# A two-block network on one core: sums of the opening moved from TensorE to the vector engine, filter directions stacked into one matmul, spectra stored later

## The chip, the cores and the metric

One core of one Trainium2 chip. The metric is the device time of one execution in microseconds, as the median of several. The core has five engines that run their own instruction streams and wait for each other by semaphores: TensorE (PE), the vector engine (DVE), ScalarE (ACT), GpSimd (POOL), and the sync engine (SP), which here only issues transfers.

## The reference

The kernel computes a first block and then two more mixer layers on x of 256 x 2048. Of the first block this matters, all in float32:

```
mod = silu(c) @ w_ada + b_ada                       # 2048 x 12288: 12 groups of 1024 columns
sh1, sc1, g1, sh2, sc2, g2 = split(mod, 6)
h = x * (1 + sc1) + sh1
z = h @ w_in + b_in                                  # 2048 x 9216
z_u, z_v, z_h, z_g = split(z, ...)
# hyena filters, from constants and small weights alone
f = sin(freq * (feats @ w1 + b1)); f = sin(freq * (f @ w2 + b2))      # 256 x 64
f = (f @ w3).reshape(256, 2 directions, 2 orders, 1024) * window
k_spec = rfft of forward and reversed backward filter, for each order
```

The rest (gating, long convolutions with k_spec, MLP, two further layers) is untouched.

## The kernel before, in words

**Opening.** x needs sh1 and sc1, and these are groups 0 to 3 of mod. A group is read in 16 *chunks* of 128 x 1024 (512 KB), so the opening has chunks 0 to 63, and 64 to 191 follow beside the weights. Chunk j is multiplied with one column of silu(c) and added to an accumulator on the vector engine (`add_chunk`, L1050); some chunks (`PE_CHUNKS`) are summed on TensorE instead with single-column matmuls (`sum_chunk`, L630), and the first of a group on ScalarE. `reduce_chunks(i)` (L616) sums a group's accumulator over partitions on TensorE, and `bias(i)` makes it mod. Chunks lie in 8 slots up to chunk 31 and in 6 slots up to 63; the sync engine issues chunk j when the slot's previous chunk has been used, and everything behind it in its program waits with it.

**Filters.** Beside that, two sine layers (`sine_layer`, L1108, and a Sin on ScalarE), then the last layer: `both(0)` and `both(1)` (L1124) make the sum and the difference of the weights of the two directions on 64 partitions, 16 hidden-layer matmuls multiply (L663), `windowed(i)` (L1128) multiplies with the window, 16 groups of matmuls (L682) make the spectra, ScalarE copies them to `ksb` and POOL writes them in eight pieces of 512 KB to `kscr` in DRAM (L2254), from where they are read when the long convolutions need them. `wait_filters` makes the first short convolution wait for all eight, because it writes where they lay.

**Weights.** All weight matrices come as *halves* of 128 x 8 x 128 floats. ScalarE rounds half h to float32r (`hi(h)`, L1761), the vector engine makes the remainder (`lo(h)`, L1038), TensorE multiplies 8 *k tiles* a half, each as two matmuls (L586 with the rounded weights on x's two parts, L590 with the remainder). A column of w_in is 16 k tiles. The first three columns go by turns: k tiles 0 to 7 of each, with `reduce_chunks(3)` behind k = 4, then, in the order of `SECOND`, k tiles 8 to 15, whose x tiles wait for groups 2 and 3. Behind that, column after column: in step i the vector engine does two `lo`, `add_halves(i)` (L1189), for the first 24 columns a short convolution, and one `add_chunk`.

Of the kernel before, what the change touches and what calls it, by code (L numbers as in the profile page):

```python
# [15 lines left out]
P = 128  # L16
# [90 lines left out]
for _i in range(2):  # L107
# [29 lines left out]
PE_CHUNKS = (2, 4, 10, 18, 25, 57)  # L137
# [4 lines left out]
SUMS = [("chunk", 2), ("chunk", 4), ("chunk", 10), ("group", 0), ("chunk", 18), ("chunk", 25), ("group", 1),  # L142
        ("group", 2), ("chunk", 57), ("group", 3)] + [("group", i) for i in range(4, 12)]
# [42 lines left out]
def n_rest(k):  # L186
# [7 lines left out]
    "ada0 ada1 ada2 ada3 ada4 ada5 ada6 ada7 fin dft hw3 scr0 scr1 scr2 scr3 khat ws0 ws1 out "  # L194
# [11 lines left out]
    "fmm sine sin fwin both spmm spec "  # L206
# [49 lines left out]
def _build(nc, ctx, d, out):  # L256
# [6 lines left out]
    s_scr = (s.scr0, s.scr1, s.scr2, s.scr3)  # L263
# [58 lines left out]
    w3 = BFf[0:64, 0:4096]  # L322
# [5 lines left out]
    w2 = small[0:64, 320:384]  # L328
    hb = small[0:64, 384:387]
    ha, hn, h1, h2 = (small[0:64, 512 + 256 * i:768 + 256 * i] for i in range(4))  # L330
# [85 lines left out]
    n_ada = {17: 4, 33: 5, 49: 6, 65: 7}  # L416
# [64 lines left out]
    def wait_filters(w):  # L481
        for scr in s_scr:
            w.wait_ge(scr, 32)
# [14 lines left out]
    def sync_program(e):  # L498
# [31 lines left out]
        e.dma_start(w2, d["hy_w2"]).then_inc(s.fin, 16)  # L530
        e.dma_start(hb, d["hy_b"]).then_inc(s.fin, 16)
# [12 lines left out]
        w.wait_ge(s.fmm, 18)  # L544
# [11 lines left out]
        for h in range(H_M2[0]):  # L556
            weights(h + 7)
            paced = h < H_WO + 16 or h >= H_M1[0]
            if h % 2 and paced and at < 192:
                chunk(at)  # L560
                at += 1
# [10 lines left out]
    def tensor_program(e):  # L572
# [79 lines left out]
        w.wait_ge(s.fin, 64)  # L652
        e.matmul(ps[4][0:64, 0:256], w1, feats, start=True, stop=True).then_inc(s.fmm, 1)
        w.wait_ge(s.sin, 1)
        e.matmul(ps[4][0:64, 0:256], w2, h1, start=True, stop=True).then_inc(s.fmm, 1)
        sum_chunk(2)
        sum_chunk(4)
        w.wait_ge(s.sin, 2)
        for i in range(16):
            n, tt = i // 2, i % 2  # L660
            w.wait_ge(s.both, n // 4 + 1)
            w.wait_ge(s.fwin, i - 2)
            e.matmul(ps[3 + i % 3][:], h2[:, tt * P:tt * P + P], w3_both[n // 4][:, n % 4 * 512:n % 4 * 512 + 512],  # L663
                     start=True, stop=True).then_inc(s.fmm, 1)
            if i == 2:
                sum_chunk(10)
            if i == 8:
                reduce_chunks(0)
            if i == 10:
                sum_chunk(18)  # L670
            if i == 13:
                sum_chunk(25)
        reduce_chunks(1)
        w.wait_ge(s.dft, 16)
        w.wait_ge(s.fwin, 16)
        for i in range(16):
# [358 lines left out]
    def vector_program(e):  # L1035
# [71 lines left out]

        def sine_layer(i):  # L1108
            w.wait_ge(s.fin, 64)
            w.wait_ge(s.fmm, i + 1)  # L1110
            w.wait_ge(s.sin, i)
            sine.up(e.tensor_scalar(ha, ps[4][0:64, 0:256], hb[:, i:i + 1], hb[:, 2:3], ALU.add, ALU.mult))
            w.wait_ge(s.sine, sine.n)
            sine.up(e.tensor_scalar(hn, ha, 1.0 / TWO_PI, MAGIC, ALU.mult, ALU.add))
            w.wait_ge(s.sine, sine.n)
            sine.up(e.tensor_scalar(hn, hn, MAGIC, None, ALU.subtract))
            for c in (C1, C2, C3):
                w.wait_ge(s.sine, sine.n)
                sine.up(e.scalar_tensor_tensor(ha, hn, -c, ha, ALU.mult, ALU.add))
            w.wait_ge(s.sine, sine.n)  # L1120
            sine.up(e.tensor_scalar(ha, ha, 3.1415925, -3.1415925, ALU.min, ALU.max))


        def both(i):  # L1124
            w.wait_ge(s.hw3, 32)
            e.tensor_tensor(w3_both[i], w3[:, 0:2048], w3[:, 2048:4096], ALU.subtract if i else ALU.add).then_inc(s.both, 1)

        def windowed(i):  # L1128
            n, tt = i // 2, i % 2
            w.wait_ge(s.fmm, 2 + i + 1)  # L1130
            w.wait_ge(s.hw3, 32)
# [18 lines left out]
        for j in V_CHUNKS[:V_UPTO[63]]:  # L1150
            add_chunk()
            if j == 3:
                sine_layer(1)
            if j == 5:
                both(0)
            if j == 8:
                both(1)
# [8 lines left out]
            if j == 52:  # L1166
# [7 lines left out]
        for k in range(8, 16):  # L1174
            if k % 4 != 3:
                w.wait_ge(s.scale1, 2)
                w.wait_ge(s_x[k // 4], 16)
                e.tensor_scalar(XR[:, k, :], XR[:, k, :], mod[:, 16 + k:17 + k], mod[:, k:k + 1],
                                ALU.mult, ALU.add).then_inc(s.made_v, 1)
            if k >= 9:  # L1180
                made_low(k - 1)
            if k in (10, 11, 14):
                lo((10, 11, 14).index(k) + 4)
# [91 lines left out]
        for i, n in enumerate(N_IN):  # L1275
# [24 lines left out]
            add_chunk()  # L1300
            if i == 2:
# [456 lines left out]
    def scalar_program(e):  # L1758
# [61 lines left out]
        for k in range(8, 16):  # L1820
            if k % 4 == 3:
                make_tile(k)
            if k >= 9:
                high(k - 1)
            if k in (10, 11, 14):
                hi((10, 11, 14).index(k) + 4)
        high(15)

# [411 lines left out]
    def gpsimd_program(e):  # L2240
# [10 lines left out]

        for m in range(8):
            w.wait_ge(s.spec, 2 * m + 2)
            e.dma_start(kscr[m // 4, m % 4], ksb[:, m % 4, :]).then_inc(s_scr[m % 4], 16)  # L2254
            if m in (4, 5):
                made_low(3 * m - 11)
        for k in (7, 10, 13):
# [266 lines left out]
```

## Time and profile before

| | |
|---|---|
| median of 3 runs | 2688.38 us (2687.2 to 2692.71) |
| profiled execution | 2686.84 us, its span 2684.8 us |
| mean granted TensorE clock | 0.982 |
| TensorE busy | 2567.2 us, 96% of the span |
| vector engine busy | 1988.4 us, 74% |
| ScalarE, POOL busy | 1393.1 us, 802.2 us |
| transfers | 534.60 MB, mean 199 GB/s |

The span runs from the first to the last instruction. Busy time of an engine is the union of its instructions; what lies between them is waiting, or time in which its sequencer works. Matmuls are pipelined, so their ends are modelled, and TensorE that shows as busy all the time need not be at its peak.

### The profile page before, as it was taken

What the parts mean: (1) busy time and instruction counts of PE and PEld (TensorE: products, weight loads), DVE (VectorE), ACT (ScalarE), POOL (GpSimd) and SP (SyncE); (2) the same over time, 40 slices, a digit from 0 to 9 for tenths busy, and PEclk for the clock granted to TensorE, in tenths of its full rate; (3) what the DMA queues carried; (4) which work ended last, traced back from release to release, by engine and by line L of the source; (5) the groups of instructions that cost most, each with busy time, mean ns of one, the idle gap of its engine ahead of it and who ended that gap; (6) DMA issues with size and microseconds to landing.
All of it is one profiled execution on the core that took longest, in us unless ns stands there. A gap on an engine that the chain in (4) does not pass through costs nothing.

```text
span 2684.8 us, 42882 instructions
## 1 busy us (share of the span) xinstructions
PE 2567.2 (96%) x16652; PEld 2334.2 (87%) x16652; DVE 1988.4 (74%) x2574; ACT 1393.1 (52%) x2180; POOL 802.2 (30%) x764
## 2 busy tenths in 40 slices
PE   7799999999998999999999989999899999999979
PEld 4588888888986888888888879999789999999978
DVE  6779777768788785546555679898758788888855
ACT  0344334444455444435544466776556666766653
POOL 0100002002134410001111338875104556666630
PEclk9899999999999999999999989999999999999989
DMA  8978766787865886556555534444455444444434
GB/s 299 371 260 282 246 210 210 255 275 247 290 237 172 283 281 219 185 172 201 190 190 190 189 108 157 158 149 154 138 172 166 143 149 156 151 150 156 148 100 155
DMA packets 146770, 534.60 MB, mean 199 GB/s; under 512 B 16679, under 2 KB 16840, under 8 KB 146248
## 3 DMA queue, kind: packets, MB, share of 16 engines
q1 hardware_dynamic: 143320, 520.33, 57.4%
q0 software_dynamic: 3248, 11.54, 1.3%
q8 instruction: 132, 2.16, 0.3%
q14 instruction: 70, 0.57, 0.1%
HBM read 525.51 MB, written 6.29 MB: 198 GB/s over the span
## 4 chain that ended last, share of the span: by engine, by line
PE 67%; DVE 14%; issue 7%; ACT 6%; DMA 5%; POOL 1%; SPq 0%; DVEq 0%; ACTq 0%; POOLq 0%
PE ps L586 30%; PE ps L590 20%; PE ps L588 5%; PE ps L589 5%; DVE wl L1042 5%; DMA ring<-in_w_ada 3%; ACT wh L1764 2%; DMA AF<-in_w_ada 2%; DVE ps L1513 1%; PE ps L648 1%; PE ps L979 1%; PE ps L725 1%; PE ps L737 1%; DVE misc L1063 1%; DVE BF L1663 1%
## 5 line engine op out<-in xcount | busy, mean ns | idle before, releaser
L1042 DVE TENSOR_TENSOR wl<-ring,wh 128x1024 fp32r<-128x1024 f32 x784 | 1034.3, 1333 | 372.1 <-ACT wh L1764 371.6
L590 PE MATMUL ps<-A,wl 128*128 128x256 f32 x4480 | 1263.9, 282 | 0.0
L1764 ACT CAST wh<-ring 128x1024 fp32r<-128x1024 f32 x784 | 812.1, 1043 | 362.9 <-PE ps L590 329.7
L590 PEld LDWEIGHTS ps<-A,wl 128*128 128x128 f32 x4480 | 857.5, 191 | 0.4
L586 PE MATMUL ps<-A,wh 128*128 128x512 f32 x2176 | 775.0, 400 | 17.8 <-DVE A L1046 7.4
L588 PE MATMUL ps<-A,wh 128*128 128x256 f32 x2304 | 674.6, 293 | 17.6 <-DVE A L1046 11.9
L586 PE MATMUL ps<-B,wh 128*128 128x512 f32 x1792 | 638.2, 400 | 21.9 <-DVE wl L1042 7.4
L589 PE MATMUL ps<-A,wh 128*128 128x256 f32 x2304 | 654.4, 284 | 0.0
L586 PEld LDWEIGHTS ps<-A,wh 128*128 128x128 f32 x2176 | 411.8, 189 | 117.7 <-DVE wl L1042 9.7
L590 PE MATMUL ps<-B,wl 128*128 128x256 f32 x1792 | 503.6, 281 | 0.0
L588 PEld LDWEIGHTS ps<-A,wh 128*128 128x128 f32 x2304 | 444.3, 193 | 20.6 <-issue 12.6
L589 PEld LDWEIGHTS ps<-A,wh 128*128 128x128 f32 x2304 | 444.5, 193 | 1.2
L586 PEld LDWEIGHTS ps<-B,wh 128*128 128x128 f32 x1792 | 339.3, 189 | 103.2 <-issue 10.1
L590 PEld LDWEIGHTS ps<-B,wl 128*128 128x128 f32 x1792 | 341.2, 190 | 0.5
L2245 POOL TENSOR_TENSOR B<-tmpA,B 128x256 fp32r<-128x256 f32 x80 | 74.5, 931 | 524.5 <-ACT B L2001 448.6
L2393 POOL TENSOR_TENSOR misc<-misc 128x256 f32<-128x256 f32 x192 | 204.2, 1063 | 44.6 <-ACT misc L2054 21.6
L2431 POOL TENSOR_TENSOR BF<-BF 128x256 f32<-128x256 f32 x128 | 155.2, 1212 | 110.6 <-ACT BF L2180 68.0
L2180 ACT ACTIVATE BF<-BF 128x256 f32<-128x256 f32 x256 | 94.4, 417 | 139.7 <-DVE BF L1653 139.7
L2433 POOL TENSOR_TENSOR BF<-BF 128x256 f32<-128x256 f32 x128 | 148.3, 1159 | 0.0
L1063 DVE SCALAR_TENSOR_TENSOR XR<-ring,cnd,XR 128x1024 f32<-128x1024 f32 x75 | 98.6, 1314 | 37.9 <-DMA ring<-in_w_ada 37.7
L1653 DVE TENSOR_TENSOR BF<-misc 128x512 f32<-128x512 f32 x128 | 121.3, 948 | 4.3 <-POOL BF L2433 3.8
L1063 DVE SCALAR_TENSOR_TENSOR misc<-ring,cnd,misc 128x1024 f32<-128x1024 f32 x62 | 82.3, 1328 | 43.7 <-DMA ring<-in_w_ada 42.7
(252 smaller groups left out, 2213.5 us busy)
## 6 DMA issues: line engine op xcount, KB each, us to landing
ring<-in_w_m SPq DMA_DIRECT2D x256, 512.0 KB, 4.5
ring<-in_hgrn_w_in SPq DMA_DIRECT2D x160, 512.0 KB, 3.8
ring<-in_w_ada SPq DMA_DIRECT2D x146, 512.0 KB, 6.6
ring<-in_w_in SPq DMA_DIRECT2D x144, 512.0 KB, 5.2
ring<-in_conv_w_in SPq DMA_DIRECT2D x96, 512.0 KB, 3.9
AF<-in_w_ada SPq DMA_DIRECT2D x46, 512.0 KB, 7.4
ring<-in_w_ab SPq DMA_DIRECT2D x32, 512.0 KB, 5.5
ring<-in_w_o SPq DMA_DIRECT2D x32, 512.0 KB, 5.3
```

The costliest lines, as they stand in the source:

```text
L586: e.matmul(dst.rearrange("p (a t) -> p a t", a=2), hi, x, start=first, stop=False)
L588: e.matmul(dst, hi, x[:, 0, :], start=first, stop=False)
L589: e.matmul(dst, hi, x[:, 1, :], start=False, stop=False)
L590: return e.matmul(dst[:, 0:256], lo, x[:, 0, :], start=False, stop=last)
L1042: e.tensor_tensor(low[:], ring[SLOT[h]][:], hi[:].bitcast(F32), ALU.subtract).then_inc(s.lo, 1)
L1063: chunks.up(e.scalar_tensor_tensor(acc, wt, cnd[:, k:k + 1], acc, ALU.mult, ALU.add))
L1653: e.tensor_tensor(E[li % 2].rearrange("p (k n h) -> p k n h", k=2, h=2 * h), inc, ref, ALU.subtract).then_inc(dif, 1)
L1764: e.copy(wh[h % NSPLIT][:], ring[SLOT[h]][:]).then_inc(s.hi, 1)
L2180: e.activation(side, side, ACT.Exp, scale=2.0 * a - 1.0).then_inc((s.exp0, s.exp1)[u], 1)
L2393: padd.up(e.tensor_tensor(pa, pa, ptmp[padd.n % NTMP], ALU.add))
L2431: e.tensor_tensor(sides(BF, at(u, 10 + x), h, h), sides(BF, at(u, 1), h, 256 + h), sides(BF, ev, h, 256 + h), ALU.mult).then_inc(kq, 1)
L2433: e.tensor_tensor(sides(BF, at(u, 13 + x) + h, h, -h), sides(BF, at(u, 0) + h, h, -h), sides(BF, ev + h, h, 256 - h), ALU.mult).then_inc(k ...
```

## The change

Five things, all in the opening and the first columns:

1. TensorE sums chunks 2 and 3 alone; chunks 4, 10, 18, 25 and 57 go to the vector engine and 3 leaves it.
2. The last filter layer takes the weights of the two directions stacked on 128 partitions (two loads of 64 partitions), with the second sine layer made twice, once with its sign turned in the lower half; so sum and difference come out of the matmul and `both` is gone. The weights are loaded behind chunk 5 and the window behind chunk 7.
3. Spectra get eight places of their own, and POOL writes them out when the vector engine has done chunk 60. The sync engine's wait for the last hidden-layer matmul ahead of x's second half is gone.
4. In the second round the x tiles and their casts stand in front of the weight halves, and the order of k tiles is another; `lo(3)` stands behind chunk 63.
5. No chunk is added in columns 0 to 2, two are in columns 24 to 26. The mask cast moves from column 2 to 12, the reduction of group 4 from column 17 to 20.

```diff
-PE_CHUNKS = (2, 4, 10, 18, 25, 57)
+PE_CHUNKS = (2, 3)
...
-SECOND = [(0, 8), (0, 9), (1, 8), (1, 9), (0, 10), (1, 10), (2, 8), (2, 9), (2, 10)]
-SECOND += [(b, k) for k in range(11, 16) for b in range(3)]
+SECOND = [(0, 8), (0, 9), (0, 10), (1, 8), (1, 9), (1, 10), (0, 11), (1, 11), (2, 8), (2, 9), (2, 10), (2, 11)]
+SECOND += [(b, k) for k in range(12, 16) for b in range(3)]
+
+def chunks_behind(i):
+    return 0 if i < 3 else 2 if 24 <= i < 27 else 1
...
-    w3 = BFf[0:64, 0:4096]
+    w3 = BFf[:, 0:2048]
...
-    w3_both = [XR[0:64, 8:16, :].rearrange("p a b -> p (a b)"), w3[:, 2048:4096]]
-    ksb = BFf[:, 0:4096].rearrange("p (u x) -> p u x", u=4)
+    ksb = [BFf[:, 1024 * m:1024 * m + 1024] for m in range(4)]
+    ksb += [win[:, i, :] for i in range(2)] + [hw[:, i, 0:1024] for i in range(2)]
...
-            if j == 3:
-                e.dma_start(w3, d["hy_w3"]).then_inc(s.hw3, 16)
-                e.dma_start(win, d["k_window"]).then_inc(s.hw3, 16)
+            if j == 5:
+                for i in range(2):
+                    e.dma_start(w3[64 * i:64 * i + 64], d["hy_w3"][:, 2048 * i:2048 * i + 2048]).then_inc(s.hw3, 16)
+            if j == 7:
+                e.dma_start(win, d["k_window"]).then_inc(s.win, 16)
...
-        w.wait_ge(s.fmm, 18)
         rows_in(2)
         rows_in(3)
...
+            w.wait_ge(s.sin, 2 + n // 4)
             w.wait_ge(s.fwin, i - 2)
-            e.matmul(ps[3 + i % 3][:], h2[:, tt * P:tt * P + P], w3_both[n // 4][:, n % 4 * 512:n % 4 * 512 + 512],
-                     start=True, stop=True).then_inc(s.fmm, 1)
+            e.matmul(ps[3 + i % 3][:], (h2 if n < 4 else h2_diff)[:, tt * P:tt * P + P],
+                     w3[:, n % 4 * 512:n % 4 * 512 + 512], start=True, stop=True).then_inc(s.fmm, 1)
...
-            if j in (56, 59, 61, 62):
-                lo((56, 59, 61, 62).index(j))
+            if j in (56, 59, 61):
+                lo((56, 59, 61).index(j))
+        lo(3)
...
-            add_chunk()
-            if i == 2:
+            for _ in range(chunks_behind(i)):
+                add_chunk()
+            if i == 12:
                 w.wait_ge(s.dft, 32)
                 e.tensor_copy(masks[:], maskf).then_inc(s.masks, 1)
...
+        for k in (1, 4, 7):
+            made_low(k)
+        w.wait_ge(s.chunk, V_UPTO[60])
         for m in range(8):
             w.wait_ge(s.spec, 2 * m + 2)
-            e.dma_start(kscr[m // 4, m % 4], ksb[:, m % 4, :]).then_inc(s_scr[m % 4], 16)
+            e.dma_start(kscr[m // 4, m % 4], ksb[m]).then_inc((s.scr0, s.scr1)[m % 2], 16)
```

TensorE's program from its first instruction to the spectra, before. The x16 rows with `cnd` are chunk sums (two here), those with `ones` reductions, the 128x512 rows the hidden layer:

```order
L655 MATMUL ps<-BF 64x256
L637 MATMUL ps<-cnd,AF 128x1 x16
L663 MATMUL ps<-XR,BF 128x512 x3
L637 MATMUL ps<-cnd,AF 128x1 x8
L663 MATMUL ps<-XR,BF 128x512 x5
L663 MATMUL ps<-BF 128x512
L626 MATMUL ps<-ones,misc 128x1 x8
L663 MATMUL ps<-BF 128x512 x2
L637 MATMUL ps<-cnd,AF 128x1 x8
L663 MATMUL ps<-BF 128x512 x3
L637 MATMUL ps<-cnd,AF 128x1 x8
L663 MATMUL ps<-BF 128x512 x2
```

And the same stretch in the changed kernel:

```order
L665 MATMUL ps<-BF 128x256
L647 MATMUL ps<-cnd,AF 128x1 x16
L674 MATMUL ps<-BF 128x512 x9
L636 MATMUL ps<-ones,misc 128x1 x8
L674 MATMUL ps<-BF 128x512 x7
L686 MATMUL ps<-BF,misc 128x256 x4
L636 MATMUL ps<-ones,misc 128x1 x8
```

The sums of chunks 10, 18 and 25 between the hidden layer's matmuls are gone, and group 1's reduction stands behind the first of the spectra.

POOL's program from its first work on, before (`kscr` is the spectra's store, `A<-XR,A` the low part of an x tile):

```order
L2254 DMA kscr<-BF 128x1024 x5
L2245 ISA
L2245 TENSOR_TENSOR A<-XR,A 128x256
L2254 DMA kscr<-BF 128x1024
L2245 TENSOR_TENSOR A<-XR,A 128x256
L2254 DMA kscr<-BF 128x1024 x2
L2245 TENSOR_TENSOR A<-XR,A 128x256 x3
```

And in the changed kernel:

```order
L2263 ISA
L2263 TENSOR_TENSOR A<-XR,A 128x256 x3
L2275 DMA kscr<-BF 128x1024 x8
L2263 TENSOR_TENSOR A<-XR,A 128x256 x2
```

The eight writes stand together, with three low parts ahead of them and two behind.

## Rows read from the trace of the kernel before

**Rows 1.** The page, the span in 40 slices: busy tenths of TensorE.
```profile
PE   7799999999998999999999989999899999999979
```

**Rows 2.** Stretches: busy PE, PEld, DVE, ACT, POOL; then granted clock, DMA share, GB/s.
```profile
12.00:15.00 3.00, 3.00 (x15) 3.00 (x15) 2.02 (x3) 0.00 (x0) 0.00 (x0) 1.00 1.09 224
...
50.00:58.00 8.00, 8.00 (x22) 4.92 (x22) 5.68 (x10) 0.00 (x0) 0.00 (x0) 1.00 0.03 6
...
80.00:118.00 38.00, 28.29 (x129) 24.12 (x127) 20.82 (x24) 17.87 (x34) 6.14 (x9) 0.91 1.02 404
118.00:132.00 14.00, 7.17 (x24) 5.94 (x24) 13.69 (x14) 1.53 (x2) 1.17 (x2) 0.50 0.93 340
...
203.00:287.00 84.00, 84.00 (x485) 73.17 (x484) 78.75 (x107) 36.78 (x44) 0.00 (x0) 1.00 0.83 282
287.00:306.00 19.00, 19.00 (x103) 16.61 (x102) 13.95 (x20) 7.33 (x11) 0.55 (x1) 1.00 0.67 229
```

**Rows 3.** The chain that ended last: start, length, what.
```profile
53.39 3.52 PE ps L637 x16
56.92 3.79 DMA AF<-in_w_ada
...
132.39 0.77 PE ps L586
```

**Rows 4.** Vector engine in order of time: start, length, line, operation, tiles.
```profile
23.07 1.28 DVE L1063 SCALAR_TENSOR_TENSOR misc<-AF,cnd,misc 128x1024 f32<-128x1024 f32 x1 [6.11 <-DMA AF<-in_w_ada]
24.27 2.28 DVE L1126 TENSOR_TENSOR XR<-BF 64x2048 f32<-64x2048 f32 x1
...
36.82 1.28 DVE L1063 SCALAR_TENSOR_TENSOR misc<-AF,cnd,misc 128x1024 f32<-128x1024 f32 x1
...
38.62 1.28 DVE L1063 SCALAR_TENSOR_TENSOR misc<-AF,cnd,misc 128x1024 f32<-128x1024 f32 x1
40.00 1.28 DVE L1063 SCALAR_TENSOR_TENSOR misc<-ring,cnd,misc 128x1024 f32<-128x1024 f32 x1
...
60.73 1.29 DVE L1063 SCALAR_TENSOR_TENSOR misc<-AF,cnd,misc 128x1024 f32<-128x1024 f32 x1 [4.84 <-DMA AF<-in_w_ada]
...
130.92 1.22 DVE L1042 TENSOR_TENSOR wl<-ring,wh 128x1024 fp32r<-128x1024 f32 x1
```

**Rows 5.** Vector engine's groups, 20 to 136 us: busy, mean ns, idle before, releasers.
```profile
L1063 DVE SCALAR_TENSOR_TENSOR misc<-AF,cnd,misc 128x1024 f32<-128x1024 f32 x35 | 45.3, 1294 | 24.9 <-DMA AF<-in_w_ada 23.8 <-DVE misc L1063 0.5
L1063 DVE SCALAR_TENSOR_TENSOR misc<-ring,cnd,misc 128x1024 f32<-128x1024 f32 x17 | 21.8, 1281 | 5.8 <-DMA ring<-in_w_ada 4.9
...
L1058 DVE TENSOR_SCALAR misc<-ring,cnd 128x1024 f32<-128x1024 f32 x1 | 0.8, 752 | 0.9 <-DMA ring<-in_w_ada 0.9
```

**Rows 6.** TensorE in order of time; two passes a matmul in the opening.
```profile
26.69 5.45 PE L663 MATMUL ps<-XR,BF 64*128 64x512 f32 x6 [1.31 <-DVE XR L1126]
...
76.53 24.57 PE L682 MATMUL ps<-BF,misc 128*128 128x256 f32 x104 [1.07 <-DVE BF L1132]
...
122.72 3.55 PE L637 MATMUL ps<-cnd,AF 128*128 128x1 f32 x16 [13.50 <-DMA AF<-in_w_ada]
...
137.65 0.63 PE L586 MATMUL ps<-A,wh 128*128 128x512 f32 x1
...
138.68 0.40 PE L586 MATMUL ps<-A,wh 128*128 128x512 f32 x1
...
147.25 0.50 PE L586 MATMUL ps<-A,wh 128*128 128x512 f32 x1 [1.07 <-DVE wl L1042]
...
157.70 0.50 PE L586 MATMUL ps<-A,wh 128*128 128x512 f32 x1 [2.08 <-DVE misc L1191]
...
168.76 0.50 PE L586 MATMUL ps<-A,wh 128*128 128x512 f32 x1 [0.80 <-DVE wl L1042]
```

**Rows 7.** Transfers from 80 to 118 us: POOL's queue, and its writes' landing.
```profile
q0 software_dynamic: 1008, 3.67, 23.7%
...
kscr<-BF POOLq DMA_DIRECT2D x7, 512.0 KB, 7.2
```

More of the change, by code:

```diff
@@ L140 @@
 V_UPTO = [sum(v <= j for v in V_CHUNKS) for j in range(192)]
-SUMS = [("chunk", 2), ("chunk", 4), ("chunk", 10), ("group", 0), ("chunk", 18), ("chunk", 25), ("group", 1),
-        ("group", 2), ("chunk", 57), ("group", 3)] + [("group", i) for i in range(4, 12)]
+SUMS = [("chunk", j) for j in PE_CHUNKS] + [("group", i) for i in range(12)]
 SUMMED = {x: i + 1 for i, x in enumerate(SUMS)}
-SECOND = [(0, 8), (0, 9), (1, 8), (1, 9), (0, 10), (1, 10), (2, 8), (2, 9), (2, 10)]
-SECOND += [(b, k) for k in range(11, 16) for b in range(3)]
+SECOND = [(0, 8), (0, 9), (0, 10), (1, 8), (1, 9), (1, 10), (0, 11), (1, 11), (2, 8), (2, 9), (2, 10), (2, 11)]
+SECOND += [(b, k) for k in range(12, 16) for b in range(3)]
+def chunks_behind(i):
+    return 0 if i < 3 else 2 if 24 <= i < 27 else 1
 NDVE = 31 - NPOOL - NPE
@@ L204 @@
     "ones sig cnd gb fill chunk adared mod scale1 masks "
-    "fmm sine sin fwin both spmm spec "
+    "fmm sine sin fwin spmm spec "
     "hmade_v hmade_a ev pre zin zh uv gate "
@@ L327, in _build @@
     w1 = small[0:33, 256:320]
[L328 to L330 removed]
+    w2 = [small[0:64, 320 + 64 * i:384 + 64 * i] for i in range(2)]
+    w2_twice = small[0:64, 320:448]
+    hb = small[:, 448:451]
+    flip = small[:, 452:453]
+    ha, hn, h1, h2, h2_diff = (small[:, 512 + 256 * i:768 + 256 * i] for i in range(5))
     dft = misc[:, 0:2048].rearrange("p (a k) -> p a k", a=8)
[L333 to L334 removed]
+    ksb = [BFf[:, 1024 * m:1024 * m + 1024] for m in range(4)]
+    ksb += [win[:, i, :] for i in range(2)] + [hw[:, i, 0:1024] for i in range(2)]
     zh = lambda i: BF[:, i, :]
@@ L481, in wait_filters @@
     def wait_filters(w):
-        for scr in s_scr:
-            w.wait_ge(scr, 32)
+        w.wait_ge(s.scr0, 64)
+        w.wait_ge(s.scr1, 64)
     def wait_lo(w, k, op):
@@ L558, in sync_program @@
             paced = h < H_WO + 16 or h >= H_M1[0]
-            if h % 2 and paced and at < 192:
-                chunk(at)
-                at += 1
+            if h % 2 and paced:
+                for _ in range(chunks_behind(h // 2 + 1) if h < H_AB else 1):
+                    if at < 192:
+                        chunk(at)
+                        at += 1
         for h in range(H_M2[0] + 7, NH):
@@ L1095, in vector_program @@
         for i in range(2):
+            e.memset(flip[64 * i:64 * i + 64], 1.0 - 2.0 * i).then_inc(s.ones, 1)
+        for i in range(2):
             for c in (0, 257):
@@ L1165, in vector_program @@
                 scale_plus_one(0)
-            if j == 52:
+            if j == 55:
                 bias(2)
@@ L1169, in vector_program, with make_tile @@
                 made_low((0, 2, 3, 5, 6)[(j - 50) // 2])
-            if j in (56, 59, 61, 62):
-                lo((56, 59, 61, 62).index(j))
+            if j in (56, 59, 61):
+                lo((56, 59, 61).index(j))
+        lo(3)
         bias(3)
         scale_plus_one(1)
[L1174 to L1183, printed above, removed]
+        def make_tile(k):
+            w.wait_ge(s.scale1, 2)
+            w.wait_ge(s_x[k // 4], 16)
+            e.tensor_scalar(XR[:, k, :], XR[:, k, :], mod[:, 16 + k:17 + k], mod[:, k:k + 1],
+                            ALU.mult, ALU.add).then_inc(s.made_v, 1)
+        make_tile(8)
+        make_tile(9)
+        made_low(8)
+        make_tile(10)
+        make_tile(12)
+        made_low(9)
+        make_tile(13)
+        make_tile(14)
+        lo(4)
+        made_low(11)
+        lo(5)
+        made_low(12)
+        made_low(14)
+        lo(6)
         made_low(15)
@@ L1819, in scalar_program @@
         hi(3)
[L1820 to L1826, printed above, removed]
+        high(8)
+        high(9)
+        high(10)
+        make_tile(11)
+        high(11)
+        hi(4)
+        high(12)
+        high(13)
+        hi(5)
+        high(14)
+        make_tile(15)
         high(15)
+        hi(6)
         def hyena():
```

68 lines of the change are left out of this document (27 added, 41 removed).

## Prediction, made before the changed kernel ran

> **What bounds the kernel now.** The page comes first: its slices show TensorE short of full in the first three and at one place in the middle [rows 1]. So a gain can only reach the end as an earlier start of the weight matmuls, since behind it TensorE has no gap to speak of (84.00 us busy of 84.00 from 203 to 287) [rows 2]. The chain of waits says what leads up to that start: additions of w_ada chunks on the vector engine, their transfers and, in one place, a chunk's sum on TensorE with a transfer right behind it, until the first weight matmul at 132.39 [rows 3]. I then read the vector engine in order of time. It begins chunk 5 at 23.07 and ends `lo(2)`, for which TensorE waits, at 130.92 + 1.22, about 132.1 [rows 4]. In these 109.0 us it idles for chunks: 23.8 + 4.9 + 0.9 us by releaser in the groups of 20 to 136, less the 6.1 us that end at 23.07, makes 23.5 us [rows 4, 5]. What is left, 85.5 us, is work and small gaps.
>
> Where the 23.5 us come from: first, from 50 to 58 the transfers stand nearly still, at 6 GB/s [rows 2]. Chunk 26 goes into the slot of chunk 18, and the sync engine waits in front of it. TensorE sums chunk 18 in program order, behind 11 hidden-layer matmuls (5.45 us for three); the sum runs from 53.39 for 3.52 us, and the transfer begins at 56.92 and is used at 60.73, for which the vector engine idles 4.84 us [rows 3, 4, 6]. Chunk 33 waits for chunk 25's sum in the same way. Second, from 80 to 118 the transfers run full, at 404 GB/s, and 3.67 MB of them are spectra going out (seven of the eight writes), 23.7% of the engines' time [rows 2, 7]. The vector engine's waits behind 86 fall into that stretch.
>
> **The change, part by part.** *Start.* I take the queue to be served in order. Chunk 5 now stands ahead of the filter weights, chunks 6 and 7 come behind them and then the window; so the bytes that were ahead of chunk 5, plus two chunks, are ahead of the window's end. A chunk is 0.524 MB, at 404 GB/s 1.30 us. The window lands at 23.07 + 2.6 = 25.7, chunk 8 at 27.0. By then chunks 4 to 7 and the second sine layer, which runs on 128 partitions instead of 64 with as many elements in each, are done in the engine's present idle time.
>
> *Work of the vector engine from there to `lo(2)`.* From the 85.5 us come off: chunks 5, 6 and 7, already done (3 x 1.38, the pitch from 38.62 to 40.00), 4.1; the two `both` at 2.2 of pitch each, 4.4; one window multiply, 0.4 (36.82 to 38.62 is 1.80 with a window, against 1.38); three partial sums of biases, 0.5. Added are chunks 10, 18, 25 and 57, which TensorE no longer takes: 4 x 1.38 = 5.5. Result 81.6 us [rows 4]. Without any wait `lo(2)` ends at 27.0 + 81.6 = 108.6.
>
> *Waits for transfers that stay.* No TensorE chunk is left in a slot behind chunk 3, and the spectra wait for chunk 60, so both causes are gone. But the slots hold the queue back to the vector engine's pace, and then six other transfers (two of x, four weight halves) are issued between chunks 40 and 52. Lower bound: chunk 40 is issued when chunk 34 is done. Chunks 8 to 30 cost 15 x 1.80 + 7 x 1.38 + 0.5 = 37.2, to 64.2; three more make 68.3. Then 22 chunks and six others at 1.30 and 2.5 us from issue to first byte (my estimate: 3.79 for a chunk into an idle queue [rows 3], less its 1.30) put chunk 61 at 107.2; the vector engine alone would begin it 2.3 us before 108.6, at 106.3. So at least 0.9 us. Upper bound: all six exposed, 7.8 us. Six slots are 8.3 us of vector work, which covers a landing time of some 4 us and about as much of the six; between the ends I take 3.0. The first weight matmul then starts at 108.6 + 3.0 + 0.3 = 111.9 instead of 132.39: **20.5 us earlier**.
>
> *TensorE in the opening.* The hidden layer stays 16 matmuls of 512 columns, now over 128 rows. Windows come two to three chunks, 2.5 us apart, more than the 1.8 us of a matmul, so the vector engine sets this pace. The spectra then take 24.57 / 13 = 1.89 each, 30.2, and two reductions 5.5: from 64.2 to about 100 [rows 6]. The cover is the vector engine's chain, which needs until 112; without it each microsecond there would count.
>
> *The first two rounds of weights.* `reduce_chunks(3)` comes behind 15 k tiles as before; chunk 63 is done 4 us after the start, in time. Before, the second round waited 1.07 us at 147.25 for a weight half [rows 6]. The new order puts two more casts and a tile in front of that half's cast on ScalarE, about 1 us, and gives TensorE one more k tile (84.00 us for 485 / 2 of them, 0.35) and the next ones to do meanwhile. I count 0, with 0.4 us either way. The 2.07 us wait at 157.70 for `add_halves(0)` stays: the same order on both engines leads to it.
>
> *Chunks 64 to 66 moved.* They leave the first three w_in columns (1.28 us each, the first of a group somewhat less), so `lo(9)`, for which TensorE waited 0.80 us at 168.76, is some 3 us earlier: **0.8 us** [rows 4, 6]. They come back one each in columns 24 to 26, where the vector engine is busy 13.95 of 19 us [rows 2]; 3 x 1.28 = 3.8 us more fit. Price without cover: 3.8 us.
>
> *Spectra last.* POOL issues its eight writes from chunk 60 on, about 105 to 110. With x, three weight halves, a table and the last chunks they are some 15 items or 20 us of queue, done by about 130. The first short convolution waits for all of them; it stands behind the addition that TensorE awaits at 157.70, 25 us behind the first matmul, so at 137. Hidden, with 7 us to spare. Behind the writes on POOL stand only low parts 10 and 13, wanted behind 120.
>
> **Clock.** From 118 to 132 the granted clock is 0.50 [rows 2], the lower level of 1.2 GHz: TensorE had idled 13.50 us before 122.72, and a weight matmul takes 0.63 us at 137.65 and 0.40 at 138.68 [rows 6]. In the changed kernel it idles from about 100 to 112 and starts at the lower level again. The 6 us at that level cost it 6 x (1 - 0.40 / 0.63) = 2.2 us; they can be less or more, so 1.5 us either way go into the range, nothing into the sum. The Trainium skill, "TensorE: Matmul & The Clock Gate", Part 1, says that the default is the throttled state and activity releases it; by that rule no pause costs more than the first start already does here.
>
> **A rule for the filter weights.** The load of 64 partitions goes slowly: 224 GB/s at 12 to 15 [rows 2], against 404 later. Now there are two loads, one to either 64 partitions. Together they could take 2.5 us less than one after the other at the old rate. The queue is in order, so I take the latter. The Trainium skill, "SBUF — State Buffer", Door 1, says that partitions 0 to 63 reach half of the ports and 64 to 127 the other half; by it each alone is slow and only both at once are fast, which leaves the same two ends.
>
> **Sum.** 2684.8 - 20.5 - 0.8 = 2663.5 span; the execution took 2686.84, 2.0 more than its span, so 2665.5. It lies 1.5 under the median of the runs, which is forecast at 2688.38 - 21.3 = **2667.1 us**. Everything behind the w_in columns moves as a block, because it hangs on semaphores alone and TensorE is full there.
>
> **Rivals.**
> 1. *Transfers stay the bound.* At the rate of 118 to 132 (340 GB/s, 1.54 us an item) the 60 items from chunk 8 to 61 end at 27.0 + 92.4 = 119.4 and the first matmul comes at 122: gain 10.3 + 0.8, time 2677.3. For: at full rate the margin is small. Against: there the slots came back late, and it was not for want of rate.
> 2. *Both filter loads go at once:* 2664.6. For: they reach all partitions now. Against: the order.
> 3. *Doubled chunks stall columns 24 to 26:* up to 3.8 us, 2670.9. For: two slots only. Against: 5 us idle there.
> 4. *Slower than before: spectra too late.* A write took 7.2 us to land at the median, several at once [rows 7]. If they went one at a time, 58 us from 108, they would end at 166 where the short convolution wants them at 137: 29 us lost, 2696. It decides from 50 us in all, 6.3 us a write. Against: seven went out in 38 us with all else moving.
> 5. *The gain fails:* the vector engine takes on 5.5 us of chunks and the waits reappear whole, 2688. Against: each had a cause that is removed.
>
> **Chances.** Forecast as summed 0.68; rival 1 0.11; 2 0.09; 3 0.07; 4 0.02; 5 0.03. The range takes in stalls of 0.9 to 7.8, the clock, rivals 2 and 3 and the near part of 1: 2661.5 to 2675.5. Under 0.2% (5.4 us) a change of this kernel can't be told from none: faster 0.95, same 0.03, slower 0.02.
>
> **What would show it.** Right: first weight matmul at 109 to 115; no pause of the transfers at 50 to 58; under 5 us of waits for chunks on the vector engine from 27 on; the writes behind 104; no gap of TensorE in the first columns; and the same length from first weight matmul to the end within 2 us. Wrong: long idle times ahead of chunk additions between 85 and 110, a wait at the first short convolution, or the lower clock lasting well over 7 us.

## The result, and the profile after

The changed kernel takes 2665.28 us (median of 4 runs, 2663.59 to 2666.47) beside 2688.59 us of the kernel before on the same chip (4 runs, 2687.2 to 2692.71): ratio 0.9908, 95% interval 0.9893 to 0.9922. The forecast was 2667.1. The profiled execution has a span of 2664.0 us, 20.8 less than before. Two later comparisons of the same kernel, on two different chips, gave 0.9926 (0.9905 to 0.9946) and 0.9933 (0.9915 to 0.995), so the gain is 15 to 23 us by the three medians.

The number is right, but not all of its parts. The page of the changed kernel, TensorE's busy tenths in 40 slices:

```profile
PE   5799999999999999999999989999899999999979
```

The first slice is emptier than in [rows 1], because sums of chunks have left TensorE: it is busy for 38.4 of the first 66.6 us, where it was for 47.6 of 67.1. The chain of waits between 18 and 118 us, in shares of these 100 us:

```profile
by line: DVE misc L1067 47.4%; DMA AF<-in_w_ada 46.3%; issue 9.6%; DVE wl L1046 2.4%; DVE BF L1136 0.9%; DVEq L238 0.3%; DVE mod L1085 0.2%; DVE A L1050 0.2%; DVE mod L1081 0.1%
```

No sum on TensorE is in it any more, as [rows 3] had it. Half is the vector engine's additions, but nearly half is transfers of w_ada (a transfer counts from its issue, so 7.3 of the 46.3 us lie ahead of 18). The long ones in the chain of the whole execution say where:

```profile
10.74 17.10 DMA AF<-in_w_ada
70.30 8.42 DMA AF<-in_w_ada
80.06 8.89 DMA AF<-in_w_ada
90.29 11.89 DMA AF<-in_w_ada
```

Each lasts from issue to use. The first fills the vector engine's start; the other three follow each other closely from 70 to 102. The vector engine in order of time, the rows that answer to [rows 4]:

```profile
27.87 1.28 DVE L1067 SCALAR_TENSOR_TENSOR misc<-AF,cnd,misc 128x1024 f32<-128x1024 f32 x1 [0.52 <-DMA AF<-in_w_ada]
...
64.21 0.68 DVE L1136 TENSOR_TENSOR BF<-ps,BF 128x512 f32<-128x512 f32 x1
...
92.96 1.28 DVE L1067 SCALAR_TENSOR_TENSOR misc<-ring,cnd,misc 128x1024 f32<-128x1024 f32 x1 [1.55 <-DMA ring<-in_w_ada]
...
102.20 1.28 DVE L1067 SCALAR_TENSOR_TENSOR misc<-AF,cnd,misc 128x1024 f32<-128x1024 f32 x1 [2.40 <-DMA AF<-in_w_ada]
...
117.02 1.22 DVE L1046 TENSOR_TENSOR wl<-ring,wh 128x1024 fp32r<-128x1024 f32 x1
```

Chunk 8 begins at 27.87 (forecast 27.0), the last window multiply ends at 64.89 (64.2), and then come seven waits for chunks, from 72.41 to the one of 2.40 us at 102.20. The two groups of additions between 27 and 118.4, which answer to [rows 5], hold 5.5 + 3.5 = 9.0 us of waiting for transfers, against 3.0 in the forecast:

```profile
L1067 DVE SCALAR_TENSOR_TENSOR misc<-AF,cnd,misc 128x1024 f32<-128x1024 f32 x37 | 47.4, 1281 | 7.3 <-DMA AF<-in_w_ada 5.5
L1067 DVE SCALAR_TENSOR_TENSOR misc<-ring,cnd,misc 128x1024 f32<-128x1024 f32 x15 | 19.2, 1280 | 3.9 <-DMA ring<-in_w_ada 3.5
```

The stretches, as in [rows 2] (busy PE, PEld, DVE, ACT, POOL; granted clock, DMA share, GB/s):

```profile
15.00:20.00 5.00, 4.91 (x24) 4.82 (x23) 3.35 (x5) 0.82 (x2) 0.00 (x0) 1.00 1.04 235
27.00:58.00 31.00, 21.62 (x40) 9.11 (x40) 29.86 (x34) 1.15 (x1) 0.00 (x0) 0.72 1.03 409
...
58.00:80.00 22.00, 16.09 (x52) 13.23 (x53) 19.66 (x20) 3.07 (x5) 0.00 (x0) 0.61 0.86 304
80.00:100.00 20.00, 20.00 (x103) 17.83 (x102) 14.57 (x14) 13.74 (x28) 1.88 (x2) 1.00 1.02 404
...
118.50:121.50 3.00, 3.00 (x10) 2.57 (x11) 2.90 (x3) 0.00 (x0) 1.93 (x4) 0.53 0.99 322
121.50:144.50 23.00, 19.47 (x114) 16.48 (x113) 12.68 (x24) 9.70 (x18) 2.48 (x3) 1.00 0.97 381
```

The pause of the transfers at 50 to 58 is gone. But from 58 to 80 they run below their rate, at 304 GB/s, as they did in the kernel before, at 331. At 409 they would have moved 22 x 105 GB/s = 2.3 MB more, 4.4 chunks or 5.7 us. TensorE in order of time, every wait over 1 us up to the end of w_in, which answers to [rows 6]:

```profile
118.49 0.77 PE L596 MATMUL ps<-A,wh 128*128 128x512 f32 x1 [16.19 <-DVE wl L1046]
...
132.72 0.50 PE L596 MATMUL ps<-A,wh 128*128 128x512 f32 x1 [1.45 <-DVE wl L1046]
...
142.72 0.50 PE L596 MATMUL ps<-A,wh 128*128 128x512 f32 x1 [2.07 <-DVE misc L1202]
...
604.07 0.36 PE L598 MATMUL ps<-A,wh 128*128 128x256 f32 x1 [2.73 <-DVE A L1050]
```

The first weight matmul comes at 118.49, so 13.9 us earlier and not 20.5. The last row is the first matmul behind w_in. The kernel before had it at 625.16:

```profile
625.16 0.55 PE L588 MATMUL ps<-A,wh 128*128 128x256 f32 x1 [5.30 <-DVE A L1046]
```

These two marks and the span cut each execution into three parts, and all kernels below are read by them:

| profiled execution | first weight matmul | from there to the matmul behind w_in | rest of the span |
|---|---|---|---|
| before | 132.39 | 492.77 | 2059.6 |
| changed, three profiles | 118.49, 117.66, 117.82 | 485.58, 485.96, 484.20 | 2059.9, 2057.4, 2066.4 |

So w_in became 6.8 to 8.6 us shorter, where 0.8 was forecast. And the rest, which the change does not touch, differs by 9.0 us among three executions of the same kernel on different chips. That is why a few us in the opening are read here from traces, and not from medians.

### The profile page after: what moved, and what is told of

Same layout as the page of the kernel before. It is cut to its first block, busy times and chain, and to the rows that moved or that the text cites. A ratio compares the mean times of both kernels' runs of the same rounds, so it can differ in the third digit from the quotient of the medians.

```text
span 2664.0 us, 42756 instructions
## 1 busy us (share of the span) xinstructions
PE 2543.0 (95%) x16588; PEld 2315.2 (87%) x16588; DVE 1994.8 (75%) x2574; ACT 1396.5 (52%) x2181; POOL 817.5 (31%) x764
## 4 chain that ended last, share of the span: by engine, by line
PE 76%; DVE 10%; issue 6%; ACT 5%; DMA 2%; POOL 1%; SPq 0%; DVEq 0%; POOLq 0%; ACTq 0%
PE ps L596 34%; PE ps L600 23%; PE ps L598 6%; PE ps L599 6%; DVE wl L1046 3%; DVE misc L1067 2%; ACT wh L1776 2%; DMA AF<-in_w_ada 2%; PE ps L983 1%; PE ps L658 1%; PE ps L729 1%; PE ps L741 1%; DVE ps L1525 1%; DVE BF L1675 1%; DVE BF L1665 1%
## 5 line engine op out<-in xcount | busy, mean ns | idle before, releaser
L2263 POOL TENSOR_TENSOR B<-tmpA,B 128x256 fp32r<-128x256 f32 x80 | 83.4, 1042 | 508.3 <-ACT B L2019 433.6
L2072 ACT ACTIVATE misc<-misc,vec 128x256 f32<-128x256 f32 x192 | 87.2, 500 | 7.3 <-POOL misc L2412 7.3
```

## The experiments

Four questions were open. Is it the queue of transfers, its order and its lead, that sets the opening, and where? (The expectations call this theory Q, and its rival, that the vector engine's own work sets it, V.) Do the moved chunks explain the shorter w_in (theory M), and if so by which mechanism? Does the new second round matter? Is the order of the spectra's writes needed? Each kernel is the changed one with one edit, except the last two, which combine edits. Two are the changed kernel itself, run again as a yardstick.

> The changed kernel once more, unchanged, as the yardstick for the others of this call. Both theories: span near 2664.0, first weight matmul near 118.5, TensorE idle some 2.7 us at 601 to 604. If the 5.8 us gained behind the first weight matmul were chance in how waits and the clock fall, this span would differ from 2664.0 by several microseconds; if it is of the program, by under 1.

> The changed kernel again, as the yardstick of this call. All theories: first weight matmul at 117.5 to 119, time 2662 to 2669.

They gave 2667.49 us (before 2687.38) and 2670.32 us (before 2685.62), the second 1.3 over what was expected. The spans are 2661.0 and 2668.4 for 2664.0, so the span as a whole is not reproduced within 1 us; what is reproduced is w_in, 485.96 and 484.20 us for 485.58. The vector engine's waits for chunks from 27 on, 9.0 us in the first profile, are 7.5 in each of these two.

**Six other transfers earlier.** x and the weight halves went out between chunks 40 and 52; now between 30 and 35.

```diff
-            if j in (40, 42):
-                rows_in((j - 40) // 2)
-            if j in (46, 48, 50, 52):
-                weights((j - 46) // 2)
+            if j in (30, 31):
+                rows_in(j - 30)
+            if j in (32, 33, 34, 35):
+                weights(j - 32)
```

> The changed kernel with the two x loads and the four weight halves issued behind chunks 30 to 35 instead of 40 to 52. Theory Q (the queue sets the start of the weights: it is held to the vector engine's pace from 58 to 80, 304 GB/s against 409, and pays for the six transfers afterwards): the six fill the stretch from 58 to 80, whose rate goes to about 400, the vector engine's waits of 8.4 us fall to 2 to 4, first weight matmul at 112 to 114 instead of 118.5, time 4.5 to 6 us less than the changed kernel. Theory V (the vector engine's own work sets it, the waits are small ones of other causes): waits stay over 6 us, under 1.5 us gained.

2667.64 us, ratio 0.9926 (0.991 to 0.9943). Its stretch of 58 to 80, and its first weight matmul:

```profile
58.00:80.00 22.00, 16.81 (x49) 13.11 (x50) 18.36 (x19) 2.91 (x4) 0.00 (x0) 0.54 1.03 409
```

```profile
114.31 0.76 PE L596 MATMUL ps<-A,wh 128*128 128x512 f32 x1 [11.34 <-DVE wl L1046]
```

The rate is full, the vector engine's waits for chunks, 7.5 to 9.0 us in the changed kernel, are 2.5 + 1.1 = 3.6 us here, and the start comes 3.4 to 4.2 us earlier. So it was the lead of the transfers in that stretch. The median shows none of it, beside 2667.49 of the changed kernel on the same chip: this profile's rest is 2065.7 us, at the long end of the spread above.

**A chunk's sum back on TensorE.** Chunk 18 is summed there again, behind the eleventh hidden-layer matmul.

```diff
-PE_CHUNKS = (2, 3)
+PE_CHUNKS = (2, 3, 18)
...
                 reduce_chunks(0)
+            if i == 10:
+                sum_chunk(18)
```

> The changed kernel with chunk 18 summed on TensorE again, behind the hidden layer's eleventh matmul. Theory Q: chunk 26, which takes its slot, is issued only behind that sum, near 51 to 55 instead of 43, the transfers pause for some 6 to 8 us, and the first weight matmul comes 4 to 7 us later, although the vector engine has 1.4 us less to do. Theory V: the first weight matmul comes 0 to 1.4 us earlier.

2666.5 us, 0.9917 (0.9896 to 0.9937). The sync engine's queue, where six issues take until 53.28 because one of them waits for chunk 18's sum, and the stretches:

```profile
41.38 11.90 SPq L516 DMA_DIRECT2D AF<-in_w_ada  x6
```

```profile
50.00:58.00 8.00, 8.00 (x16) 3.86 (x15) 7.72 (x11) 0.00 (x0) 0.00 (x0) 0.53 0.65 215
58.00:80.00 22.00, 15.51 (x49) 12.58 (x49) 20.60 (x22) 2.91 (x4) 0.00 (x0) 0.69 1.03 412
```

The pause comes back, at 215 GB/s, and yet the first weight matmul comes at 116.92, 0.7 to 1.6 us *earlier*. Theory Q had it 4 to 7 us later; that did not happen. The transfers lose 8 x 194 GB/s = 1.6 MB at 50 to 58, but at 58 to 80, where the changed kernel loses 2.3 MB, they lose nothing; and the vector engine has one addition less (1.38). So this pause cost nothing here, and taking chunk 18 from TensorE, one of the pieces of the change, gained nothing at the start.

**Work given back to the vector engine, early and late.** Two unused additions, the size of one `both` each, behind chunks 9 and 12 in one kernel, and in four halves behind chunks 43 and 46 in the other.

```diff
+            if j in (9, 12):
+                w.wait_ge(s.hw3, 32)
+                e.tensor_tensor(XR[0:64, 8:16, :].rearrange("p a b -> p (a b)"), w3[0:64], w3[0:64], ALU.add)
```

```diff
+            if j in (43, 46):
+                for x in range(2):
+                    e.tensor_tensor(XR[0:64, 8 + 4 * x:12 + 4 * x, :].rearrange("p a b -> p (a b)"),
+                                    small[0:64, 512:1536], small[0:64, 512:1536], ALU.add)
```

> The changed kernel with two additions of 64 x 2048 on the vector engine, of the size of the removed sum and difference, behind chunks 9 and 12; their result is used by nothing. Theory Q (transfers set the start of the weights): 4.4 us more work is mostly absorbed in the 7 to 8 us of waits for chunks, first weight matmul 0 to 2 us later. Theory V: 4 to 4.5 us later, with the waits as they were.

> The changed kernel with additions of the size of the two removed ones (4.4 us in all, result unused) behind chunks 43 and 46, where the vector engine waits for chunks at a full queue. The same work behind chunks 9 and 12 moved the first weight matmul by 3.1 us and left 7.25 us of waits. Theory S (work ahead of the end of the windows delays the return of slots and so the queue as well; work in the stretch with the full queue is absorbed): 0 to 1.5 us later, waits down by 3 to 4. Theory V (work counts wherever it stands): 3 to 4.4 us later.

Early: 2671.66 us, 0.9937 (0.9916 to 0.9958), first weight matmul at 121.15. Late: 2666.86 us, 0.9936 (0.9918 to 0.9954), at 118.32. The late one's groups on the vector engine:

```profile
L1067 DVE SCALAR_TENSOR_TENSOR misc<-AF,cnd,misc 128x1024 f32<-128x1024 f32 x37 | 48.1, 1300 | 4.0 <-DMA AF<-in_w_ada 2.4
L1067 DVE SCALAR_TENSOR_TENSOR misc<-ring,cnd,misc 128x1024 f32<-128x1024 f32 x15 | 19.2, 1279 | 1.9 <-DMA ring<-in_w_ada 1.4
...
L1160 DVE TENSOR_TENSOR XR<-BF 64x1024 f32<-64x1024 f32 x4 | 5.2, 1342 | 0.0
```

Late, 5.2 us of added work replace 3.7 to 5.2 us of waiting (7.5 to 9.0 become 3.8) and the start stays where it was, within 0.7 us. Early, 4.6 us of work put off the start by 2.7 to 3.5, between what the two theories expected; the waits are 7.3 us, hardly less than without it. So at chunks 9 and 12 the vector engine's work sets the time, since the slots come back at its pace and what it loses there delays the issues too; at chunks 43 and 46 the transfers set it. Where the one gives way to the other was not tried; the first wait for a chunk behind 27.87, at 72.41, is for chunk 37.

**Spectra's writes among the low parts again.** POOL issues each write as soon as its spectrum is made.

```diff
-        for k in (1, 4, 7):
-            made_low(k)
-        w.wait_ge(s.chunk, V_UPTO[60])
         for m in range(8):
...
+            if m in (4, 5):
+                made_low(3 * m - 11)
+        for k in (7, 10, 13):
             made_low(k)
```

> The changed kernel with the eight spectra written out as soon as each is made, as in the kernel before. Theory Q: eight writes of 1.3 us join the full queue between 75 and 103, so the first weight matmul comes 8 to 10 us later, near 127 to 128, and the time is 8 to 10 us longer. Theory V: the writes are mostly hidden, the first weight matmul under 3 us later.

2678.7 us, 0.9964 (0.9952 to 0.9975), the clearest of the edits. The transfers run full and the additions wait, 9.9 + 7.6 us in these groups:

```profile
100.00:118.00 18.00, 2.76 (x13) 2.09 (x11) 12.65 (x14) 4.19 (x7) 1.84 (x3) 0.64 1.02 410
```

```profile
L1067 DVE SCALAR_TENSOR_TENSOR misc<-AF,cnd,misc 128x1024 f32<-128x1024 f32 x37 | 48.1, 1300 | 11.5 <-DMA AF<-in_w_ada 9.9
L1067 DVE SCALAR_TENSOR_TENSOR misc<-ring,cnd,misc 128x1024 f32<-128x1024 f32 x15 | 19.2, 1282 | 7.9 <-DMA ring<-in_w_ada 7.6
```

The first weight matmul comes at 127.96, 9.5 to 10.3 us later. Eight writes of 0.524 MB at 410 GB/s are 10.2 us. Postponing them is the largest of the pieces of the gain that were tried singly: 9.5 to 10.3 us, beside 2.7 to 3.5 for work of the size of the two `both` and nothing for chunk 18, of 13.9 to 14.7 us in all. The pieces need not add up, and the sums of chunks 4, 10, 25 and 57 were not put back singly.

**One chunk in each column, as before.**

```diff
-    return 0 if i < 3 else 2 if 24 <= i < 27 else 1
+    return 1
```

> The changed kernel with one chunk added in every column again, none moved to columns 24 to 26. Theory M (what was gained behind the first weight matmul comes from the chunks moved): the waits in the first columns come back (0.8 to 1 us, and a stretch at the lower clock near column 3, 1.5 us), the late chunks at the end of w_in too, so the gap at 601 grows from 2.7 to about 5.3; in all 4 to 6 us longer. Rival C (it comes from elsewhere or from chance): under 1.5 us longer, the gap at 601 as it was. My prediction's own term was 0.8 us.

2671.55 us, 0.994 (0.9917 to 0.9964). The start is the same (117.86), w_in takes 489.23 us, 3.3 to 5.0 more. TensorE waits at two places where the changed kernel does not, or less (2.73 at 604.07):

```profile
152.71 0.50 PE L596 MATMUL ps<-A,wh 128*128 128x512 f32 x1 [1.73 <-DVE wl L1046]
...
607.09 0.55 PE L598 MATMUL ps<-A,wh 128*128 128x256 f32 x1 [4.44 <-DVE A L1050]
```

That makes 1.73 + 1.71 = 3.4 us. The vector engine's additions between 200 and 625 us, in the changed kernel and in this one:

```profile
L1067 DVE SCALAR_TENSOR_TENSOR XR<-ring,cnd,XR 128x1024 f32<-128x1024 f32 x62 | 81.4, 1313 | 1.7 <-DMA ring<-in_w_ada 1.6
```

```profile
L1067 DVE SCALAR_TENSOR_TENSOR XR<-ring,cnd,XR 128x1024 f32<-128x1024 f32 x59 | 77.7, 1317 | 25.8 <-DMA ring<-in_w_ada 25.7
L1062 DVE TENSOR_SCALAR XR<-ring,cnd 128x1024 f32<-128x1024 f32 x4 | 3.0, 750 | 3.7 <-DMA ring<-in_w_ada 3.7
```

The chunks that come late in this kernel, 29.4 us of waiting, come in time in the changed one. The sync engine's queue shows how, in the changed kernel and then in this one:

```profile
503.17 0.33 SPq L516 DMA_DIRECT2D ring<-in_w_ada  x1
504.31 2.36 SPq L531 DMA_DIRECT2D ring<-in_w_in  x2
509.23 0.33 SPq L516 DMA_DIRECT2D ring<-in_w_ada  x1
```

```profile
501.53 1.46 SPq L531 DMA_DIRECT2D ring<-in_w_in  x2
503.04 0.45 SPq L516 DMA_DIRECT2D ring<-in_w_ada  x1
508.22 2.26 SPq L531 DMA_DIRECT2D ring<-in_w_in  x2
```

Here the chunk is issued in one go with the two halves in front of it, 0.05 us behind them, and is the one wanted next. In the changed kernel it goes out a column ahead of its use: chunk 64 is still issued before the columns, but nobody adds one in the first three, so from then on the issues are one ahead of the additions.

**One in each column, but one ahead.** To part the two effects, the sync engine issues chunk 65 right behind 64, and each column adds one.

```diff
-    return 0 if i < 3 else 2 if 24 <= i < 27 else 1
+    return 1
...
-        at = 65
+        chunk(65)
+        at = 66
```

> One chunk in every column again, as in the run where that was undone, but the sync engine issues chunk 65 right behind 64 and stays one chunk ahead of the vector engine for all columns. In the changed kernel it is one ahead by a side effect: columns 0 to 2 add nothing, but chunk 64 is issued before them all the same. Theory A (that lead is what took away the late chunks): chunk waits of the vector engine from column 16 to the m1 weights fall from 26.7 to under 5 us, the stretch around 601 goes from 51.3 back to 49.0 to 49.6 us; the first columns keep about 1 us of their loss. Rival L (the lightened first columns did it, by lasting distance between the engines): late waits stay over 20 us.

2667.6 us, 0.9923 (0.9907 to 0.9938), start 117.67, w_in 486.71. Its additions between 200 and 625 wait for nothing:

```profile
L1068 DVE SCALAR_TENSOR_TENSOR XR<-ring,cnd,XR 128x1024 f32<-128x1024 f32 x58 | 76.3, 1315 | 0.0
```

So the lead of one chunk takes away all late chunks. TensorE's wait behind w_in is 2.73 us again, so it gives 4.44 - 2.73 = 1.7 us. The wait in the first columns stays:

```profile
152.62 0.50 PE L597 MATMUL ps<-A,wh 128*128 128x512 f32 x1 [1.86 <-DVE wl L1047]
```

So the first columns without chunks give the other 1.7 to 1.9. (The difference of the whole w_in, 489.23 - 486.71 = 2.5 us, holds some change of the clock besides.)

**The old second round.** `SECOND`, and with it the order on the vector engine and ScalarE, as before.

```diff
-SECOND = [(0, 8), (0, 9), (0, 10), (1, 8), (1, 9), (1, 10), (0, 11), (1, 11), (2, 8), (2, 9), (2, 10), (2, 11)]
-SECOND += [(b, k) for k in range(12, 16) for b in range(3)]
+SECOND = [(0, 8), (0, 9), (1, 8), (1, 9), (0, 10), (1, 10), (2, 8), (2, 9), (2, 10)]
+SECOND += [(b, k) for k in range(11, 16) for b in range(3)]
```

> The changed kernel with the second round as before: weight halves between the x tiles and their casts on ScalarE and the vector engine, and the old order of its k tiles. My prediction's term: no change, 0.4 us either way, with waits of about 1.1 us at the start of the round. Rival: the new order is what the start-to-column-3 time gained (24.0 to 24.4 against 25.1 us), so that it goes back to 25 or more. Read by the length from the first weight matmul to the first k tile of column 3, with the granted clock beside it.

2665.63 us, 0.9919 (0.9903 to 0.9935). TensorE's wait for the half in the second round, beside 1.45 at 132.72 in the changed kernel:

```profile
132.26 0.50 PE L596 MATMUL ps<-A,wh 128*128 128x512 f32 x1 [1.07 <-DVE wl L1046]
```

w_in takes 485.27 us, as with the new order (484.20 to 485.96), and from the first weight matmul to column 3 it is 23.9 us beside 24.2 to 24.6. The new order gains nothing and waits 0.4 us longer at this place.

**What they point to.** The early six together with the old second round, and the same with chunk 57 on TensorE behind the spectra, where it idles.

```diff
-PE_CHUNKS = (2, 3)
+PE_CHUNKS = (2, 3, 57)
...
+        sum_chunk(57)
```

> The changed kernel with the six other transfers issued behind chunks 30 to 35 and the second round in the old order. Opening: first weight matmul at 114 to 115 as in the run with the six alone, 0.3 to 0.5 us less in the second round. If what is gained up to there reaches the end, the median is 4 to 5 us under the changed kernel's of this call; if something takes it back behind the w_in columns (the run with the six alone showed no gain in its median), it is within 1.5 us of it.

> The kernel of the run before, and chunk 57 summed on TensorE behind the spectra, where TensorE idles anyway. Its slot goes to chunk 63. The vector engine has 1.4 us less to do in the stretch where it is busy throughout: first weight matmul 1 to 1.4 us earlier than in the run before, near 113, if the vector engine is the bound there; unchanged if chunks still come late there, and later if chunk 63 waits for the sum.

2663.86 us, 0.9917 (0.9903 to 0.9931), and 2662.34 us, 0.9919 (0.9903 to 0.9935); the changed kernel on the same chip 2670.32, 0.9933 (0.9915 to 0.995). The intervals overlap, so by time alone none is shown to beat the changed kernel. Their starts are earlier, at 114.51 and 113.48. In the second, TensorE sums chunk 57 at 103.78 in its idle time:

```profile
103.78 3.54 PE L647 MATMUL ps<-cnd,AF 128*128 128x1 f32 x16 [5.49 <-DMA AF<-in_w_ada]
113.48 0.76 PE L596 MATMUL ps<-A,wh 128*128 128x512 f32 x1 [6.15 <-DVE wl L1047]
```

## Why the prediction came out right, step by step

**The start** was forecast at 111.9 and came at 118.49, 6.6 us later. Of these, 0.7 stood already behind the last window multiply (64.89 for 64.2) and 0.5 are small gaps; the other 5.4 are waits, 8.4 us in seven rows from 72.41 to 102.20 where 3.0 were taken, more than the 7.8 given as the upper bound. The step that failed is the one under "Waits for transfers that stay". It made one balance from chunk 34 to chunk 61, and there the vector engine's low parts, late in the stretch, seem to cover the transfers. But the six other transfers end behind chunk 52, and nothing that comes later covers them. By the same rates the balance at chunk 53 reads: 68.3 + 20 items x 1.30 + 2.5 = 96.8, against 108.6 less the 16.0 us that the vector engine needs from there (118.24 - 102.20), so 92.6: 4.2 us of waiting and not 0.9. The other part lies ahead of chunk 40. The step took the queue as empty when chunk 40 is issued; but the transfers had run low (210 GB/s from 60 to 68.9), and the chunks in front of it were issued in a bunch. The sync engine issues chunks 36 and 37 here, the second at 66.11:

```profile
64.32 2.12 SPq L516 DMA_DIRECT2D ring<-in_w_ada  x2
```

Chunk 37 is used at 72.41 and the ones behind it land at some 1.3 us each, so that chunk 40, issued at 68.92, lands at 76.15, where the step has 68.3 + 2.5 + 1.30 = 72.1: 4.0 us. The two parts make 8.2 of the 8.4 us. Moving the six (waits of 3.6 us for 7.5 to 9.0, with the queue full from 58 to 100) bears both parts out together, and adding work late (waits down to 3.8, no later start) shows that it is waiting that can be filled.

The pause at 50 to 58, which the prediction puts first among the causes of waiting, costs nothing when it comes back in part, with chunk 18's sum (215 GB/s; it was 6 in the kernel before). The second cause, the spectra in a full queue, is the one that the runs bear out.

**"Everything behind the w_in columns moves as a block"** holds within the spread of the rest (2057.4 to 2066.4 for 2059.6). But the sum took w_in itself as a block too, but for 0.8 us, and it lost 6.8 to 8.6. This is the second step that failed. TensorE's waits of over 0.3 us in w_in add up to 10.0 us in the kernel before, to 6.3 in the changed one and to 9.7 in the one with one chunk in each column. So 3.4 us come from the moved chunks, half of it by a mechanism that the prediction did not see: the issues run one chunk ahead. It read the rows of the first columns, and not the waits for chunks between 200 and 625, which were there in the trace before (35.3 + 2.4 us).

The other half of the shorter w_in is the clock, argued from rows and not tried. The kernel before began its weights at the lower level:

```profile
132.40:138.40 6.00, 6.00 (x19) 5.14 (x20) 3.73 (x3) 0.00 (x0) 0.32 (x1) 0.50 0.93 355
```

In all it spent 11.5 us of w_in at that level, with a second stretch at 158.9 to 162.3, and the three profiles of the changed kernel 2.8, 4.7 and 3.2. At 1 - 0.40 / 0.63 = 0.37 us lost for each, that is an estimated 2.5 to 3.2 us. It is in part luck: with late additions, which leave these columns alone, w_in spent 9.5 us at the lower level and took 489.01 us.

**The sum** is right by luck, because the two errors cancel: 6.6 late at the start, 6.1 too little behind it (2552.4 to 2545.5 is 6.9 of gain, for 0.8). 2663.5 was forecast as the span, 2664.0 it is. In the two repeats the start is 5.8 and 5.9 late and the gain behind it 9.0 and 1.8, which makes spans of 2661.0 and 2668.4.

**Its own signs** come out mixed. Three that it named for being right hold: no pause at 50 to 58, the writes behind 104, no gap of TensorE in the first columns beyond those foreseen. Three do not: the first weight matmul was to come at 109 to 115 (118.49), the waits for chunks to stay under 5 us (9.0), and the length from there to the end to be the same within 2 us (6.9 shorter). And one that it named for being wrong, long idle times ahead of additions between 85 and 110, is there, with 2.40 us at 102.20.

**The other steps.** The hidden layer at the vector engine's pace: right, TensorE waits for window multiplies, and the spectra end at 102.30 (forecast about 100), far ahead of the start. The second round at 0 with 0.4 either way: right. The spectra's writes: issued at 116.02 (forecast 105 to 110, since chunk 60 is late too), and what reads them goes at 140.40. The vector engine's first short convolution begins at 142.71 and waits for nothing, so 2.3 us were to spare, where 7 were forecast. POOL's rows:

```profile
116.02 4.41 POOL L2275 DMA_DIRECT2D kscr<-BF  x8 [13.72 <-DVE misc L1067]
...
140.40 0.58 POOL L2285 DMA_DIRECT2D XR<-kscr  x1 [7.14 <-DMA kscr<-BF]
```

**The rivals.** Rival 1, transfers stay the bound, is half true: chunks come late from 37 to 53, by the transfers' lead and not by the rate of 340 GB/s that it assumed; it gave a start at 122. Rival 2 falls: the two filter loads ran at 235 GB/s at 15 to 20, one after the other, landing at 19.16 and 21.64 where chunks land 1.28 us apart. The Trainium skill, "SBUF — State Buffer", Door 1, gives each half of the partitions half of the ports. The trace agrees: each load alone (0.524 MB in 2.4 to 2.5 us) went at about half of the 404 to 409 of full transfers. Rival 3 falls: no wait of TensorE over 0.3 us from 142.72 to 604.07. Rival 4 falls by POOL's rows, rival 5 by the result.

## What to carry to other kernels

Where slots hold a queue back, make the balance of transfers and work at every place where foreign transfers end, not once over the whole stretch. Put foreign transfers where the slots leave the queue idle, just behind the slow consumer, and not where the stream already runs at its rate: the same six cost 3.9 to 5.4 us less waiting when they went ten and more chunks earlier. When a change moves consumers and leaves the issues alone, it changes the lead; one transfer of lead removed 29 us of the vector engine's waits for chunks here, but only 1.7 us of TensorE's.

## What the runs showed of the hardware that was not expected

TensorE can be busy throughout and yet be granted the lower level. In the changed kernel's opening (same columns as above):

```profile
68.00:72.00 4.00, 4.00 (x19) 3.82 (x18) 3.46 (x3) 0.58 (x1) 0.00 (x0) 0.50 0.86 249
72.00:76.00 4.00, 4.00 (x10) 3.19 (x11) 3.45 (x5) 0.34 (x1) 0.00 (x0) 0.50 1.03 381
76.00:80.00 4.00, 4.00 (x18) 3.46 (x17) 3.10 (x3) 0.99 (x3) 0.00 (x0) 0.88 1.02 417
```

It had idled 5.73 us before 65.04, and the granted clock comes back only within the last of these stretches. It cost nothing here, as the spectra had 16 us to spare. And how long it stays at the lower level behind the first weight matmul varies from kernel to kernel without a wait to go with it: in the kernel with late additions the clock was 0.89 from 119 to 145 and 0.94 from 145 to 175, for 0.96 and 1.00 in the changed one, with the same two waits (1.46 and 2.09 us). Its w_in took 489.01 us, 3.0 to 4.8 more than in the three profiles of the changed kernel. The early six, chunk 18 and the spectra among the low parts show such a second stretch as well. What decides it stays open.
